# Products of ones in TensorE's waits, attention and gating steps spread over weight tiles, a gate bias loaded early

## What is computed

```python
def first_block(x, c, ctx, ...):          # depth 2
    # layer 0: macaron FFN on x and ctx, mixer, macaron FFN on x
    x = macaron_half_ffn(x, ...); xc = macaron_half_ffn(xc, ...)
    y = even_mixer(h, hx, ...)            # neighbourhood attention (8 heads, 512 keys) and a gated
                                          # chunkwise recurrence (4 heads, 2 directions, 4 chunks)
    x = macaron_half_ffn(x + gt * y, ...)
    # layer 1: FFN, spatial gating, FFN
    x = macaron_half_ffn(x, ...)
    x = x + gt * spatial_gating(h, ...)   # 8 groups of a 128x128 token product, with a bias
    return rms_norm(macaron_half_ffn(x, ...), final_g)

def second_block(x, ...):                 # depth 2
    for l in range(2):
        mix = even_mixer_2(x, ...) if l % 2 == 0 else odd_mixer(x, ...)   # 16 heads each, blocks of 128
        x = layer_norm_2(ALPHA * x + mix, ...)
        x = layer_norm_2(ALPHA * x + routed_moe(x, ...), ...)             # 16 experts, 2 for a token
    return x
```

## Time and profile before

| | us |
|---|---|
| median of 3 runs | 2582.94 |
| lowest, highest of them | 2581.94, 2587.4 |
| the profiled execution | 2592.51 |
| its span from first to last instruction | 2590.7 |

### The profile page before, as it was taken

The page is one execution under the profiler, slowest core; times in us unless marked ns, Lnnn a source line. Parts: engine busy times, 40 slices in busy tenths (PEclk is TensorE's granted clock), DMA queues, the critical chain, the costliest instruction groups (busy, mean ns, idle before and its releaser), DMA issues.

```text
span 2590.7 us, 34009 instructions
## 1 busy us (share of the span) xinstructions
PE 2452.1 (95%) x14244; PEld 2102.6 (81%) x14244; DVE 1719.2 (66%) x2263; ACT 1194.5 (46%) x1520; POOL 98.7 (4%) x187
## 2 busy tenths in 40 slices
PE   5999999899999999999999998989999899899998
PEld 1788888767789999998899997867777787778776
DVE  5897776652656656655556655568878775688786
ACT  3222212333434444445444444456656644566665
POOL 0111111010000000000000000000000000000000
PEclk8999999998869999999899998999999896999999
DMA  6677887322114554455334452238877630388774
GB/s 257 216 243 255 267 265 260 131 76 95 66 35 161 179 195 163 175 193 217 139 131 164 178 203 99 82 128 332 333 270 297 252 114 33 114 330 321 287 301 181
DMA packets 80387, 501.19 MB, mean 193 GB/s; under 512 B 9604, under 2 KB 10708, under 8 KB 28496
## 3 DMA queue, kind: packets, MB, share of 16 engines
q1 hardware_dynamic: 59120, 423.66, 44.4%
q0 software_dynamic: 21088, 75.01, 9.1%
HBM read 497.58 MB, written 1.05 MB: 192 GB/s over the span
## 4 chain that ended last, share of the span: by engine, by line
PE 69%; DVE 16%; ACT 9%; issue 3%; DMA 2%; DVEq 0%; ACTq 0%; SPq 0%; POOL 0%; POOLq 0%
PE bank L394 67%; DVE wl L1913 7%; ACT wh L1304 6%; DVE macc L1949 2%; ACT s L1394 1%; DVE f L2074 1%; PE bank L577 1%; DMA raw<-in_wstream 1%; DVE s L2065 1%; DMA raw<-in_wmod 1%; PE bank L1198 1%; DVE rs L1973 1%; DVE hl L2049 1%; ACT H L1403 0%; DVE tmp L2042 0%
## 5 line engine op out<-in xcount | busy, mean ns | idle before, releaser
L1913 DVE TENSOR_TENSOR wl<-raw,wh 128x2048 fp32r<-128x2048 f32 (+1 forms) x430 | 903.8, 2107 | 404.7 <-ACT wh L1304 402.1
L1304 ACT ACTIVATE wh<-raw 128x2048 fp32r<-128x2048 f32 (+1 forms) x430 | 755.0, 1763 | 366.4 <-PE bank L394 354.3
L394 PE MATMUL bank<-hh,wh 128*128 128x258 f32 (+2 forms) x2200 | 700.8, 319 | 43.9 <-DVE wl L1913 23.5
L394 PE MATMUL bank<-hh,wl 128*128 128x258 f32 (+2 forms) x2200 | 681.5, 310 | 0.0
L394 PE MATMUL bank<-hl,wh 128*128 128x258 f32 (+2 forms) x2200 | 680.1, 309 | 0.0
L394 PEld LDWEIGHTS bank<-hh,wh 128*128 128x128 f32 x2200 | 428.1, 195 | 72.3 <-issue 23.0
L394 PEld LDWEIGHTS bank<-hl,wh 128*128 128x128 f32 x2200 | 429.0, 195 | 18.5
L394 PEld LDWEIGHTS bank<-hh,wl 128*128 128x128 f32 x2200 | 427.4, 194 | 19.2
L394 PE MATMUL bank<-wh,hh 128*128 128x512 f32 (+1 forms) x704 | 278.4, 395 | 5.5 <-DVE hl L2825 2.8
L394 PE MATMUL bank<-wl,hh 128*128 128x512 f32 (+1 forms) x704 | 274.0, 389 | 0.0
L394 PE MATMUL bank<-wh,hl 128*128 128x512 f32 (+1 forms) x704 | 274.0, 389 | 0.0
(11 more groups left out here) (424 smaller groups left out, 2716.8 us busy)
## 6 DMA issues: line engine op xcount, KB each, us to landing
raw<-in_wstream SPq DMA_DIRECT2D x393, 1024.0 KB, 5.0
mring<-in_wmod POOLq DMA_DIRECT2D x128, 512.0 KB, 4.6
raw<-in_wmod SPq DMA_DIRECT2D x8, 1024.0 KB, 9.1
X<-in_xT SPq DMA_DIRECT2D x1, 2048.0 KB, 12.3
bias<-in_nabias POOLq DMA_DIRECT2D x16, 128.0 KB, 2.5
c_sglg<-in_sglg POOLq DMA_DIRECT2D x1, 1024.0 KB, 5.2
c_sglb<-in_sglb POOLq DMA_DIRECT2D x1, 1024.0 KB, 7.5
out<-X SPq DMA_DIRECT2D x4, 256.0 KB, 2.2
```

Of the source, the lines that this page charges most:

```text
L394: return e.matmul(out, lhsT, rhs, start=start, stop=stop, skip_group_check=True)
L1304: e.activation(wh[i % NB][:, o], raw[i % NR][:, o], ACT.Copy).then_inc(*slab_high(st.split + m))
L1913: e.tensor_tensor(wl[i % NB][:, o], raw[i % NR][:, o], wh[i % NB][:, o].bitcast(F32), ALU.subtract).then_inc(*slab_low(st.split + m))
```

## The change

A helper `fill(n, cols)` is added to TensorE's program. It takes the bank that is next in turn without claiming it, waits for that bank's readers and for `ones`, and issues n float32 products of the 128x128 `ones` with `ones` repeated to `cols` columns (256 unless said). Nothing reads the result. It is called: 26 products after `first_mods`; 13 before `mixer0`; 4 before the recurrence's outer products; 1 of 128 columns in each of the 18 rounds of the loop over `outs`; 9 before the gated heads are turned; 4 before `even_mixer`, 2 before its attention and 3 after it has turned the cumulated gates; 8 before `odd_mixer`; in `odd_mixer` 2 before the projections of the last queries, 1 of 128 columns after each of the 15 attention steps between them, 2 of 128 columns after each of the next five steps and after each of two turns; in each `moe` 6 before the router and 4 before the ranks.

Steps are moved. In `gating_mixer` the first eight `gating` steps no longer stand behind the projections 14 and 15 of `sgin`, four behind each, but inside them, one after every second tile. In `even_mixer` the attention steps beside `eqb` and `ekb` stand one after every fourth tile instead of two after every eighth; ACT and DVE follow. In `mixer0` ACT and DVE place their steps of the neighbourhood attention two to every four tiles, with slabs split in quarters there (`st.fine`); TensorE's order there stays. `gateb` moves from the mixer's constants to the resident ones: POOL loads it at the start, after `lng`.

```diff
+        def fill(n, cols=T):
+            b = st.turn % 8
+            while b in st.kept:
+                b = (b + 1) % 8
+            if b in st.drain:
+                w.wait_ge(*st.drain[b])
+            w.wait_ge(dve_out, "ones")
+            out = banks[b][:, 0:cols].rearrange("p (a b) -> p a b", b=P)
+            for _ in range(n):
+                mm(out, ones[:], ones[:].unsqueeze(1).to_broadcast([P, cols // P, P]), True, True)
@@ project
                     if every and (k + 1) % every == 0:
-                        attend(1)
+                        (step or attend)(1)
@@ mixer0, TensorE
+            fill(4)
             w.wait_ge(act_out, "mv", 3)
...
                 if i >= 2:
                     numerator(i - 2)
+                fill(1, P)
             w.wait_ge(dve_out, "y", "na", 1)
             for c in range(4):
                 turn_out("mix0", Y, c)
+            fill(9)
@@ gating_mixer, TensorE
             for m in range(Z_FIRST, 16):
-                project("sgin", 1, m, T, h, act_out, "sgu", m)
-                if m > 13:
-                    for i in range(4 * (m - 14), 4 * (m - 13)):
-                        gating(i)
+                gates = iter(range(4 * (m - 14), 4 * (m - 13)))
+                project("sgin", 1, m, T, h, act_out, "sgu", m, every=2 if m > 13 else 0, step=lambda n: gating(next(gates)))
@@ even_mixer, TensorE
+            fill(2)
             st.units = attention("ev", EV, ev.a, logits, values, (4,))
...
+            fill(3)
...
             for m in range(4):
-                project("ein", 1, 6, T, h, dve_out, "eqb", m0=m)
+                project("ein", 1, 6, T, h, dve_out, "eqb", m0=m, every=4)
                 if m == 3:
                     turned(0, bank(("turn", "ev", 0), dve_out, "turn l", "ev", 0))
-                attend(2)
-                project("ein", 1, 10, T, h, dve_out, "ekb", m0=m)
+                project("ein", 1, 10, T, h, dve_out, "ekb", m0=m, every=4)
                 if m == 3:
                     turned(1, bank(("turn", "ev", 1), dve_out, "turn l", "ev", 1))
-                attend(2)
@@ odd_mixer, TensorE
                         if k in units:
                             attend(1)
+                            fill(1, P)
                             pump(1)
...
+            fill(2)
             p(3, 0, "oqc", m0=1, units=OD_UNITS)
             result.mark("h read", "oin")
             pump(100)
             pad()
-            attend(5)
+            for _ in range(5):
+                attend(1)
+                fill(2, P)
             for i in (2, 3):
                 turned(i, bank(("turn", "od", i), dve_out, "turn l", "od", i))
+                fill(2, P)
                 attend(1)
@@ moe, TensorE
+            fill(6)
             b = bank(("aff", l), act_out, "aff", l)
...
+            fill(4)
             b = bank(("rank", l), dve_out, "flag", l)
@@ the main order, TensorE
         first_mods()
+        fill(26)
...
         norm_began(1)
+        fill(13)
         mixer0()
...
+        fill(4)
         even_mixer()
...
         layer_norm(1)
+        fill(8)
         odd_mixer()
@@ mixer0, ACT
-            for m in range(1, 4):
-                taken(KC)
-                attend(4)
-            taken(KC)
-            attend(100)
+            st.fine = True
+            for n in (2, 2, 2, 2, 2, 2, 4, 4):
+                attend(n)
+                taken(4)
+            st.fine = False
@@ mixer0, DVE
-            for m in range(1, 4):
-                taken(KC)
-                attend(4)
-                keys(m)
-            taken(KC)
-            attend(100)
+            st.fine = True
+            for m in range(1, 5):
+                for _ in range(2):
+                    attend(2 if m < 4 else 4)
+                    taken(4)
+                if m < 4:
+                    keys(m)
+            st.fine = False
@@ even_mixer, DVE
-            def evac(key, m, dst, scale=None):
+            def evac(key, m, dst, scale=None, units=0):
                 taken(KC)
+                attend(units)
@@ POOL
-        for name in ("ident", "bmod", "ng", "lng"):
+        for name in ("ident", "bmod", "ng", "lng", "gateb"):
             load(name)
...
-        for name in ("mlcs", "swap", "gateb", "sel4", "mlmask", "headg"):
+        for name in ("mlcs", "swap", "sel4", "mlmask", "headg"):
             load(name)
```

More of the change, by code:

```diff
@@ L172, in program @@
     lng = const(ctx, "lng", [P, 8, KC])
+    gate_bias = const(ctx, "gateb", [P, 1])
     early = ExitStack()
@@ L625, in turn_out, with project @@
             ins.then_inc(*result("turn", name, c))
-        def project(name, chunks, c0, n, h, by, *key, m0=0, every=0):
+        def project(name, chunks, c0, n, h, by, *key, m0=0, every=0, step=None):
             for m in range(m0, m0 + chunks):
@@ L1473, in mixer0 @@
             for d in range(2):
-                act(ml.IR[:, d, :], b[32 * d:32 * d + 4, :], ACT.Identity, bias=ml.gb[32 * d:32 * d + 4, :], key=("mgate i", d))
-                act(ml.FR[:, d, :], b[64 + 32 * d:68 + 32 * d, :], ACT.Identity, bias=ml.gb[64 + 32 * d:68 + 32 * d, :],
+                act(ml.IR[:, d, :], b[32 * d:32 * d + 4, :], ACT.Identity, bias=gate_bias[32 * d:32 * d + 4, :], key=("mgate i", d))
+                act(ml.FR[:, d, :], b[64 + 32 * d:68 + 32 * d, :], ACT.Identity, bias=gate_bias[64 + 32 * d:68 + 32 * d, :],
                     key=("mgate", d - 1))
@@ L2546, in even_mixer @@
             for m in range(4):
-                evac("eqb", m, ev.qb[:, m, :], 0.125)
+                evac("eqb", m, ev.qb[:, m, :], 0.125, 1)
+                attend(1)
                 if m == 3:
                     turned(0)
-                attend(2)
-                evac("ekb", m, ev.kb[:, m, :])
+                evac("ekb", m, ev.kb[:, m, :], None, 1)
+                attend(1)
                 if m == 3:
                     turned(1)
-                attend(2)
             pad()
```

3 lines of the change are left out of this document (1 added, 2 removed).

## The result

The changed kernel takes 2605.01 us (median of 15 runs, 2593.62 to 2626.38), the kernel before, in 15 runs beside it, 2589.23 us (2567.31 to 2610.51). The ratio is 1.0078, 95% interval 1.0044 to 1.0111: slower by 0.8%, where 0.986 was expected (2547 us against the 2582.94 of the three runs then known). The profiled execution took 2598.6 us with a span of 2596.8, 6.1 us more than that of the kernel before, although its mean granted clock is higher, 0.969 against 0.953.

A forecast was written before the change was run, and what follows sets the result against it. TensorE, busy at half clock in long stretches, was taken to bound the kernel; 14 + 12 + 2.6 + 0 + 0 + 1.5 + 4.4 + 1.5 = 36 us gained, giving 2556.5 us profiled, 2547 median, range 2534 to 2569.

The forecast's parts named there:

- Gating: Gating mixer's spread steps: up to 6.8 us regained, offset by waits and one clock fall; 0 (-4 to +5).
- the neighbourhood attention: In `mixer0`: spreading leaves TensorE's order as it is and TensorE is busy throughout, so 0; the stretch stays low.
- the even mixer: Spread steps gain 5 us (0 to 10) from six low stretches, less misplaced products of ones; net 1.5 us gained.
- the odd mixer: The 37.4 us stretch comes to 20.4 at the upper clock, gain 17, less 4.9 for products; net 12 us.
- The loop over `outs`: Products of ones lift the clock; a round falls from 3.17 to 2.00 us; 14 us gained.
- the routers: In each MoE, six products fit the wait before the router; 2.2 us gained each time, 4.4 (0 to 6).
- rival A: One of the two long stretches, loop over `outs` or odd mixer, stays at the lower clock: about 2565 us; chance 0.18.
- Few rows count like standing still: In the loop over `outs`, products with four input rows seem to let the clock fall though TensorE is busy.
- Rival C: Neighbourhood attention's 581 to 601.5 comes out at the upper clock: another 9 us gained, 2538 us; chance 0.14.
- The rest of `mixer0`: Products before the outer products and gated heads fit in waits; 2.6 us (0 to 5), 1.4 from outer products.
- The starts: The 26, 13 and 8 products stay inside waits of 18.3, 6.8 and 4.7 us; 1.5 us gained together (0 to 5).
- Rival B: Products of ones in a loop without waits lift nothing; both long stretches stay at 0.50: 2591 us; chance 0.06.

The follow-up runs named there:

- gate_rows128: Changed kernel with the gating's bias product widened from one input row to 128, steps still spread: 2592.36 us, ratio 1.0029.
- rows128: Kernel before with all products of ones except the loop's, resident bias, 128 rows in gating's bias and `weights` selection products, no moved steps: 2535.57 us, ratio 0.9818.
- rows_only: Kernel before with only the gating's bias product and the two selection products of `weights` widened to 128 rows: 2551.78 us, ratio 0.9872.
- bias_only: Kernel before with only the gate bias made resident and loaded at the start: 2587.73 us, ratio on record 0.9955.
- na_back: Changed kernel with ACT's and DVE's neighbourhood attention steps and whole-slab splits as before, bias still resident: 2600.37 us, ratio 1.0058.
- after_less18: Changed kernel with the 26 products of ones after `first_mods` cut to 8: 2597.69 us, ratio 1.0062.
- best3: `rows128` without the even mixer's 4, 2 and 3 products of ones, plus an unused resident tile of 32 bytes a partition: 2546.56 us, ratio 0.9825.
- best1: `rows128` plus products of ones in the neighbourhood attention, without the even mixer's and the 2 before the odd mixer's last projections: 2545.86 us, ratio 0.9872.
- fills_only: Kernel before with all products of ones and the resident bias, none of the moved steps: 2580.39 us, ratio 0.9983.
- after: The changed kernel's first profile: profiled execution 2598.6 us.

## Why the prediction was wrong

The forecast was 36 us gained, and the first pair of profiles shows 6.1 us lost. The steps that failed are terms of the sum. Gating, put at 0, lost 10.3 us; the neighbourhood attention, put at 0, lost 5.7; the even mixer, put at 1.5 gained, lost 5.6; the odd mixer, put at 12 gained, gave 3.9; and the MoE behind its routers, in no term, lost 7.2. The loop over `outs` and the routers came out as forecast.

**The loop over `outs`: right in size, for one execution.** 52.1 us became 35.9, 16.2 gained where 15.4 were forecast (14 and the 1.4 of the outer products, which stand in the same stage), and a round takes 1.95 us where 2.00 was forecast:

```profile
714.78 0.48 PE L394 MATMUL bank<-mMR,c_sel 4*128 4x128 f32 x2
...
716.41 0.39 PE L394 MATMUL bank<-ones 128*128 128x128 f32 x2
716.73 0.48 PE L394 MATMUL bank<-mMR,c_sel 4*128 4x128 f32 x2
```

But the level is not a fixed property of the kernel. With four-row products and no product of ones in the loop it was low in three profiles of four; with one in each round it was low in one of eight. So rival A, a long stretch that stays low, is an outcome in part of the executions of one kernel, not a case by itself, and the kernel before has its luck too. The profiled execution from which the saving was counted was an ordinary one (2592.51 us at 0.953, and 66 of 73 runs are of that kind). What the forecast lacked is that the changed kernel, too, comes at several levels: its runs range from a mean clock of 0.971 to 0.957, and its second profile has the loop at 57.2 us.

**Few rows count like standing still: right in that widening them keeps the clock,** as `gate_rows128`, `rows128` and `rows_only` show. What the prediction missed in the same rows is the second price: in the earlier trace rows `weights` takes 1.06 us at the upper level for three products, where three at its own 0.22 would take 0.66. I priced a fill from full products alone and did not ask what a change of rows costs.

**Gating: the step that failed most.** Forecast 0 (-4 to +5), measured 10.3 us lost. The wait for the norm (2.25 us; 2.4 in the sum; the profile calls it issue, and DVE's norm ends at 1256.50, TensorE's first gating product starts at 1256.60) and ACT's `z` copies behind the activation were right:

```profile
DVE hl L2463 <- ACT hh L1628: 21.9, 8, 10.2
```

(DVE's waits from 1256 to 1296: total, times, longest.) Wrong was "falls to the lower level once (1.7 us)". TensorE was busy without a break from 1256.8 to 1294.3 and stayed at 0.50; with 128 rows in the same products the lower level lasts 3.4 us. (The Trainium skill, TensorE: Matmul & The Clock Gate, "Why this matters for your kernels", asks only that TensorE is kept busy without idle gaps. By that rule it would have come back to 1.00 behind the wait; 37.50 of 37.5 us busy at 0.50 disagree.) The rule that I had drawn from the loop I did not apply to the move that puts few-row products between full ones behind a wait.

**Neighbourhood attention: "0 too", measured 5.7 us lost.** I had argued that TensorE's order stays and that TensorE is busy there. The cover was thin: `kT` is made by DVE, and the finer splits delay it, 1.18 us of waiting became 1.64 + 2.33. The low stretch of 27.3 us in place of 20.5 is no proof of more, since the level there changes from run to run. The other half was right: the bias's 4.1 us came back as a wait of 4.9 us for `wl` one slab earlier. With whole splits that wait is 1.2 us, as `bias_only` and `na_back` show. At one level, 1.00, the stage takes 8.2 us more with the finer splits than without. Rival C, the attention at 1.00, came in the second profile of the changed kernel and in six other kernels, four of which have no product of ones there; it is low in six profiles of seven with the finer splits, and in four of eight with whole ones and no product of ones there. So chance has a part in it at each run, and whether the finer splits have one too is open.

**The even mixer: forecast 1.5 gained, measured 5.6 lost.** The misplaced products cost what was said: TensorE still waits 2.19 us for `e_vb` ahead of the three. The spread steps, for which I took 5 us of gain from half of six low stretches, lose: they give ACT another order, which the prediction had not looked at. The stage takes 133.0 to 139.0 us in all eight profiles that have them and 123.0 to 129.3 in all nine that don't. The chain of the changed kernel at its worst place:

```profile
1652.07 0.56 ACT E_ev L1461 x2
1652.63 0.50 ACT hh L1695
...
1653.15 0.70 DVE hl L2571
...
1654.10 2.05 PE bank L394 x8
```

The turn of the heads, for which TensorE waits, stands on ACT behind the exponentials of the attention step that was moved ahead of it. TensorE waits 3.10 us, and from within that wait (1652.8) the clock is at 0.50 for 10.2 us.

**The odd mixer: right direction, a third of the size.** Forecast 12 net, measured 3.9 (5.5 gained, 1.6 of it lost ahead of the attention). The gain of 17 was mis-sized. It took the whole stretch to be at the upper level, since it "keeps whichever level it enters with"; but the last 13.7 us fell to 0.50 although it was entered at 1.00. From 41.0 to 13.7 us at 0.50 gives back half of 27.3, 13.7 us. TensorE idles for 2.65 us of the 41.6 at 1.00, and the stage gained 5.5, so some 5.5 are left as the price of the products in this part (an estimate), and 1.6 more ahead of it: 7.1, near the upper end of the 4.9 to 7.3 that was forecast. And it is no sure gain: `after_less18` and `best3` have the products and ran 34.1 us at 0.50 there (106.3 us for the part behind the first values), while in `best1` it took 92.6.

**The rest.** Routers: 2.0 us each, 4.0 of the 4.4 forecast. The rest of `mixer0` behind the loop, 1.2 of the 2.6 forecast, gave 0.2. The starts were to give 1.5; what lies ahead of the neighbourhood attention lost 1.6. The MoE's 7.2 us (2.0 and 5.2) were in no term: the prediction had looked at what added instructions cost where they stand, and not at what they do to the code behind them. The pauses for code are a part of it alone, since the kernel before has 3.22 and 1.44 us of them and the changed one 2.77 and 3.38; the resident bias, with about 1 us for each of six groups, fits the rest. No run separates the two in the changed kernel.

Rival B, that products of ones lift nothing, is refuted by `fills_only` (loop 36.0 us, odd mixer 98.8). Its price, 2591 us, or 8 slower, lies nearest to the medians by luck: in the first profile of the changed kernel neither long stretch stays low as it has it. The profiled stages sum to 6.1 us slower. The medians say 15.8. Of the unprofiled runs only the mean clock is known, and it goes with the time (0.971 at 2594.03 us, 0.957 at 2626.34); the second profile shows what such a slower run looks like inside, but how often each stretch is low is not known. Of the 9.7 us between 6.1 and 15.8, then, no more can be said than that the profiled execution of the changed kernel was 6.4 us under its median and that of the kernel before 3.3 over its own.

## What to carry to other kernels

Before filling TensorE's gaps with dummy products, look at the rows of the products that are there: widening one-row and four-row products to 128 gave 1.3% by itself, where filling and spreading lost 0.8%. Before moving a step, ask what each engine has queued in front of the result that TensorE wants next, and whether the wait that this makes lets the clock fall in a place that can't lift it again. A saving read from one profiled execution holds for executions at the same levels; take a second profile, of the changed kernel above all, and compare stages at the same level.

## What the runs showed of the hardware that was not expected

- A float32 product of 128 columns starts 0.22 us after the one ahead at 1.00, and 0.41 us where each product has another number of input rows than the one ahead (1 and 128 in turn, `after` from 1298.81).
- TensorE busy for 37.50 of 37.5 us stayed at 0.50 with one-row products between full ones, and came back after 3.4 us with 128 rows in their place.
- One kernel's long stretches come out at 0.50 in one execution and at 1.00 in another: the loop over `outs` 52.1 and 33.3 us in two profiles of the kernel before, 35.9 and 57.2 in two of the changed one.
- TensorE pauses for 1.4 to 4.9 us at places near its branches that go with the length of its program, and goes on 1.19 to 1.49 us after a 16 KB packet of the instruction queue has ended (23 pauses in 13 profiles).
- With the gate bias resident, TensorE goes on about 1 us later after each group of experts. Why was not found.
